# Expert numbers worked out on GpSimd between its gathers, in a two-layer trunk with product-key experts

## The chip, the cores and the metric

One core of a Trainium2 chip runs the whole program. The metric is the device time of one execution in microseconds. Of the kernel before there are three timed runs: 5895.33 us is their median, 5893.27 the lowest and 5913.72 the highest.

## The reference

Two layers run over 640 tokens (128 context, 512 latent) of width 1024. Each layer mixes tokens in four branches, merges them with gates, and then runs a retrieval of experts, which is the part that matters here:

```
q    = h @ w_q                                  # 8 heads, two halves of 128 each
sc   = scores of each half against 128 keys
s_half, i_half = top_k(sc, 16)                  # per half: 16 values and their key numbers
cand = s_half[0][:, None] + s_half[1][None, :]  # 256 sums a head
top_s, top_pos = top_k(cand, 16)
eidx = i_half[0][top_pos // 16] * 128 + i_half[1][top_pos % 16]
gate = softmax(top_s)
out  = sum_k gate_k * gelu(u_tab[eidx_k] . h) * v_tab[eidx_k]
```

A token so reads 8 x 16 = 128 rows of the two tables (16384 rows, stored side by side, 8 KB a row).

## The kernel before, in words

Everything is float32. Tokens lie in five tiles of 128, tile 0 being the context; tiles 0 and 1 form chunk 0, tiles 2 to 4 chunk 1. The gates, the output projection and the expert scores are done for chunk 0 first and then for chunk 1 (second gates pass, score stretch). An expert group has 2 slots in chunk 0 and 4 in chunk 1.

A slot is one gather: one expert row for each of the 128 tokens of a tile, 1 MB, into one of up to 15 places of the ring `ring[...]` in SBUF. There are 5 x 128 = 640 slots a layer. GpSimd issues them in order (line 444), each behind a wait that its place is free: places used by TensorE come free with `pe_used`, those used by VectorE with `dve_used`. The ring has 6 places at first, more from slots 132, 236, 352, 400 and 528 on (`LATER`, line 101). Slots are used in groups (`GROUPS`, line 80): of a group VectorE forms all products with the hidden row (`products`, line 1394), ScalarE applies the gelu (line 862), VectorE multiplies the gates in (`weights`, line 1414), and the weighted sum is then made by TensorE with diagonal matrices (line 476, made by ScalarE in line 868) for all but the last slot of a group, and by VectorE for the last (`sums`, line 1426).

Before a tile's slots can be gathered, its 8 heads must be selected on VectorE. `select(t, i)` (line 1382) does part i % 4 of head i // 4: `half_tops` (the best 16 of both halves), `pair_tops` (the best 16 of 256 sums), `places` (gates' exponents, the two halves of the position, and the comparison of each with the list 0..15), `numbers` (the multiplication by the key numbers, the reduction, and the expert's number into `EI`). The last signals `ei_ok`, on which GpSimd waits once for each 16 slots.

The parts lie in the order of work as follows. Tile 0's heads come one after another, between copies of two score rounds each (lines 1464 to 1469). Tile 1's parts follow one by one behind each pair of expert groups in the second gates pass (`select(1, s)`, line 1477), while tile 0's rows are gathered and used, with weight loads on SP's queue beside them. Tile 2's parts lie in the score stretch (lines 1493 to 1502):

```
experts(AT_KEYS + hp * KEY_STEP)
if hp:     score_copy(1, hp - 1); v.drain()
if hp >= 2: select(2, hp * KEY_STEP - 4)
experts(AT_KEYS + hp * KEY_STEP + 1)
if hp >= 2: select(2, hp * KEY_STEP - 3)
```

and the last head's four parts stand together behind it (line 1507). In that stretch TensorE does the queries of a round (line 533), one expert group, the key scores of the round before (line 541) and a second expert group (lines 799 to 804). Parts of tiles 3 and 4 lie one behind each expert group of tiles 2 and 3. Places 7 to 11 of the ring are first used once the last scores are copied (`pq_s`, line 440).

Of the kernel before, what the change touches and what calls it, by code (L numbers as in the profile page):

```python
# [16 lines left out]
ALU = mybir.AluOpType  # L17
ACT = mybir.ActivationFunctionType
AX = mybir.AxisListType

P = 128
# [17 lines left out]
PH = 8  # L39
# [75 lines left out]


HOME, BEFORE = rows_in_ring()
TURN = [HOME[:n].count(HOME[n]) for n in range(TILES * SLOTS)]
TURNS = [HOME.count(s) for s in range(HOMES)]

# [41 lines left out]
def program(nc, ws, cst, tabs, masks, ppd, cvec, rowd, fing, skd, kcd, vcd, tables, xin,  # L162
            y_out, nk_out):
    with ExitStack() as ctx:
# [64 lines left out]

        KS = [A[:, 0:2048], A[:, 2048:4096], B2[:, 2048:4096], B2[:, 4096:6144], R[:, 0:2048]]  # L230
        small = Small(A[:, 6144:6144 + SMALL])
        diag = [A[:, 7424 + i * P:7424 + (i + 1) * P] for i in range(DIAGS)]
        acc = A[:, 8192:9216]
        wgt = A[:, 10368:10624]
# [86 lines left out]
        pq_q = sig("pq_q", 2 * UNITS)  # L321
        pq_sp = sig("pq_sp", 2 * UNITS)
        pq_s = sig("pq_s", 2 * UNITS, 2)
        ei_ok = sig("ei_ok", TILES * PH)
        got = [sig(f"got{b}", 16 * TURNS[b]) for b in range(HOMES)]
        g_exp = sig("g_exp", TILES)
# [69 lines left out]
        @block.gpsimd  # L396
        def _(pool):
            for l in range(0, DEPTH):
                pool.wait_ge(layer_done.sem, layer_done.at(l, 0))
                pool.memset(convh, 0.0)  # L400
                pool.memset(V[:, 5, :], 0.0).then_inc(pads.sem, 1)

                pool.wait_ge(fo_ops.sem, fo_ops.at(l, CJ))
                pool.memset(kTw[:, :, 5 * P:6 * P], 0.0).then_inc(pads.sem, 1)


                def queries(n):
                    flat = A[:, 4352:10752]
                    pool.tensor_copy(QN[0], flat[:, bass.ds(n * 1280 + 640, 512)])
                    pool.tensor_copy(QN[1], flat[:, bass.ds(n * 1280, 512)]).then_inc(qs_ok.sem, 1)  # L410


                pool.wait_ge(kq_ok.sem, kq_ok.at(l, 1))
                pool.wait_ge(ln_n.sem, ln_n.at(l, 1))
                queries(0)
                for n in range(1, TILES):
                    pool.wait_ge(qt_ps.sem, qt_ps.at(l, n))
                    queries(n)


                for n in range(TILES * SLOTS):
                    s, b = HOME[n], BEFORE[n]
                    if n % TOPK == 0:
                        pool.wait_ge(ei_ok.sem, ei_ok.at(l, n // TOPK + 1))
                    if b in PE_AT:
                        pool.wait_ge(pe_used.sem, pe_used.at(l, PE_AT[b] + 1))
                    elif b in DVE_AT:
                        pool.wait_ge(dve_used.sem, dve_used.at(l, DVE_AT[b] + 1))
                    elif s == 3:

                        pool.wait_ge(pq_s.sem, pq_s.at(l, UNITS))
                    elif s == 5:

                        pool.wait_ge(ei_ok.sem, ei_ok.at(l, PH))
                    elif s == 6:

                        pool.wait_ge(ei_ok.sem, ei_ok.at(l, 2 * PH))
                    elif s == 7:

                        pool.wait_ge(pq_s.sem, pq_s.at(l, 2 * UNITS))  # L440
                    elif s >= 12:

                        pool.wait_ge(ei_ok.sem, ei_ok.at(l, (s - 9) * PH))
                    pool.indirect_dma_start(  # L444
                        out=ring[s], out_offset=None, in_=tables[:, :],
                        in_offset=bass.IndirectOffsetOnAxis(ap=EI[:, n:n + 1], axis=0),
                    ).then_inc(got[s].sem, 16)
# [365 lines left out]
        def _(act):  # L813
# [39 lines left out]
            def experts(l, q):  # L853

                g = GROUPS[q]
                if g.place == 0:
                    act.wait_ge(ei_ok.sem, ei_ok.at(l, (g.tile + 1) * PH))
                    gates = GT[:, g.tile * SLOTS:(g.tile + 1) * SLOTS]
                    act.activation(gates, gates, ACT.Exp).then_inc(g_exp.sem, 1)
                c, w = g.slots[0] % (2 * SLOTS), len(g.slots)  # L860
                act.wait_ge(u_done.sem, u_done.at(l, q + 1))
                act.activation(gel[:, c:c + w], dots[:, c:c + w], ACT.Gelu_apprx_tanh).then_inc(u_act.sem, 1)  # L862
                act.wait_ge(wgt_ok.sem, wgt_ok.at(l, q + 1))
                for n in g.pe:
                    p, o = PE_AT[n], n % (2 * SLOTS)

                    act.wait_ge(pe_used.sem, pe_used.at(l, p + 1 - DIAGS))
                    act.activation(diag[p % DIAGS], ident, ACT.Copy, scale=wgt[:, o:o + 1]).then_inc(diag_ok.sem, 1)  # L868
# [180 lines left out]
        def _(v):  # L1049
# [35 lines left out]
            for l in range(0, DEPTH):  # L1085
# [254 lines left out]

                def pair_tops(w, t, h):

                    v.tensor_copy(w.sf, w.si)
                    v.tensor_tensor(out=w.cand.rearrange("p (a b) -> p a b", a=TOPK),
                                    in0=w.sv[:, 0, :].unsqueeze(2).broadcast_to([P, TOPK, TOPK]),
                                    in1=w.sv[:, 1, :].unsqueeze(1).broadcast_to([P, TOPK, TOPK]), op=ALU.add)
                    v.drain()
                    top16([w.cand], [w.tv], [w.ti])

                full = [P, 2, TOPK, TOPK]  # L1350

                def places(w, t, h):

                    v.tensor_scalar(out=GT[:, bass.ds(t * SLOTS + h * TOPK, TOPK)], in0=w.tv, scalar1=w.tv[:, 0:1], scalar2=None,
                                    op0=ALU.subtract)

                    v.tensor_scalar(out=w.pu[:, 0, :], in0=w.ti, scalar1=TOPK * (TOPK - 1), scalar2=None, op0=ALU.bitwise_and)
                    v.tensor_scalar(out=w.pu[:, 1, :], in0=w.ti, scalar1=TOPK - 1, scalar2=None, op0=ALU.bitwise_and)
                    v.drain()
                    v.tensor_copy(w.pf, w.pu)  # L1360
                    v.drain()
                    v.tensor_tensor(out=w.EQ, in0=w.pf.unsqueeze(3).broadcast_to(full),
                                    in1=io[:, 0:2 * TOPK].rearrange("p (c a) -> p c a", c=2).unsqueeze(2).broadcast_to(full),
                                    op=ALU.is_equal)
                    v.drain()

                def numbers(w, t, h):

                    v.tensor_tensor(out=w.EQ, in0=w.EQ, in1=w.sf.unsqueeze(2).broadcast_to(full), op=ALU.mult)
                    v.drain()  # L1370
                    v.tensor_reduce(out=w.ef, in_=w.EQ, axis=AX.X, op=ALU.add)
                    v.drain()

                    v.scalar_tensor_tensor(out=w.er, in0=w.ef[:, 0, :], scalar=float(P), in1=w.ef[:, 1, :], op0=ALU.mult, op1=ALU.add)
                    v.drain()
                    v.tensor_scalar(out=EI[:, bass.ds(t * SLOTS + h * TOPK, TOPK)], in0=w.er,
                                    scalar1=io[:, bass.ds(l + 2 * TOPK, 1)], scalar2=None, op0=ALU.add)
                    v.drain().then_inc(ei_ok.sem, 1)  # L1378

                parts = (half_tops, pair_tops, places, numbers)  # L1380

                def select(t, i):

                    if i < 4 * PH:
                        parts[i % 4](small, t, i // 4)

                def products(q):

# [239 lines left out]
```

## Time and profile before

| | |
|---|---|
| median of three runs | 5895.33 us |
| profiled execution | 5903.82 us, span 5902.0 us |
| TensorE busy | 4460.0 us (76%) |
| VectorE busy | 3760.7 us (64%) |
| ScalarE busy | 870.3 us (15%) |
| GpSimd busy | 1581.7 us (27%), 1280 gathers among it |
| gathers on the DMA engines | 1342.26 MB, 56.7% of 16 engines' span |
| loads on the DMA engines | 240.02 MB, 10.9% |
| mean granted TensorE clock | 0.875 |

Busy times are shares of the whole span, and the phases of the kernel have different limits, so the table alone does not say what a change in one phase is worth. The idle time in front of an instruction stands in brackets in the listings, with what ended it. The clock is given as a share of full speed.

### The profile page before, as it was taken

To read this page: it belongs to the slowest core of one execution; us is meant where nothing else is said; L and a number is where in the kernel's file an instruction comes from. 1 tells how busy PE (TensorE), PEld (TensorE's weight loads), DVE (VectorE), ACT (ScalarE), POOL (GpSimd) and SP (SyncE) were. 2 spreads that over 40 slices of the span, in tenths; PEclk is the share of its full clock that TensorE was granted. 3 is DMA by queue.
4 is the path that set the end of the run, shared out by engine and by line. 5 is a ranking of instruction groups with operands and counts; after the bars stand their busy time and mean duration, and the time that the engine had idled before them with its cause. 6 is when DMAs were issued, how large, how long until landed. Compare 5 with 4: busy or idle time off the path is not lost.

```text
span 5902.0 us, 46602 instructions
## 1 busy us (share of the span) xinstructions
PE 4460.0 (76%) x14496; PEld 2588.8 (44%) x14496; DVE 3760.7 (64%) x8187; ACT 870.3 (15%) x2476; POOL 1581.7 (27%) x1310
## 2 busy tenths in 40 slices
PE   5999997888755666666669999968887556666665
PEld 3766685444432222222238667854444322222222
DVE  0655316688666888886607553177885668888765
ACT  1023201111100111111110232101111001111111
POOL 0000000333312544445300000013432234444453
PEclk8999898999877788888879999989998778888887
DMA  6100143899965999999851001439998669999996
GB/s 239 58 29 1 34 146 119 337 379 373 357 232 209 421 421 421 421 420 422 334 223 50 29 1 62 146 142 363 375 366 322 233 244 421 421 421 421 420 421 287
DMA packets 226377, 1585.27 MB, mean 269 GB/s; under 512 B 26064, under 2 KB 28368, under 8 KB 46672
## 3 DMA queue, kind: packets, MB, share of 16 engines
q0 software_dynamic: 184320, 1342.26, 56.7%
q1 hardware_dynamic: 41808, 240.02, 10.9%
q8 instruction: 116, 1.90, 0.1%
q14 instruction: 133, 1.09, 0.0%
HBM read 1579.03 MB, written 3.15 MB: 268 GB/s over the span
## 4 chain that ended last, share of the span: by engine, by line
PE 42%; DMA 33%; DVE 17%; issue 3%; ACT 3%; DVEq 2%; POOL 1%; SPq 0%; ACTq 0%; POOLq 0%
DMA B<-tables,R 19%; PE ps L476 9%; DMA A<-tables,R 6%; PE ps L486 5%; PE ps L596 5%; DMA H<-tables,R 4%; DVE A L1426 4%; DVE B L1394 4%; PE ps L533 3%; DMA B<-ws 3%; PE ps L581 2%; PE ps L493 2%; PE ps L506 2%; PE ps L701 2%; PE ps L688 2%
## 5 line engine op out<-in xcount | busy, mean ns | idle before, releaser
L476 PE MATMUL ps<-B,A 128*128 128x512 f32 x1928 | 1124.1, 730 | 663.0 <-ACT A L868 662.8
L444 POOL DMA_INDIRECT B<-tables,R x716 | 859.1, 1200 | 1932.4 <-DVEq L1378 740.3
L1394 DVE SCALAR_TENSOR_TENSOR B<-B,M 128x1024 f32<-128x1024 f32 x716 | 867.2, 1225 | 292.5 <-DMA B<-tables,R 263.8
L476 PEld LDWEIGHTS ps<-B,A 128*128 128x128 f32 x1928 | 422.1, 230 | 1285.0 <-ACT A L868 788.4
L476 PE MATMUL ps<-A 128*128 128x512 f32 x896 | 524.7, 723 | 253.7 <-ACT A L868 253.7
L486 PE MATMUL ps<-H,B 128*128 128x384 f32 (+1 forms) x2048 | 595.3, 445 | 62.9 <-DMA B<-ws 42.0
L444 POOL DMA_INDIRECT A<-tables,R x356 | 443.5, 1246 | 681.8 <-PE ps L476 372.0
L486 PEld LDWEIGHTS ps<-H,B 128*128 128x128 f32 x2048 | 400.0, 196 | 254.5 <-DMA B<-ws 47.0
L1394 DVE SCALAR_TENSOR_TENSOR A<-A,M 128x1024 f32<-128x1024 f32 x356 | 433.4, 1224 | 116.3 <-DMA A<-tables,R 103.9
L862 ACT ACTIVATE T<-T 128x2 f32<-128x2 f32 (+1 forms) x448 | 91.6, 204 | 2531.5 <-DVEq L1396 2531.5
L476 PEld LDWEIGHTS ps<-A 128*128 128x128 f32 x896 | 201.3, 234 | 534.8 <-ACT A L868 307.9
L476 PE MATMUL ps<-H,A 128*128 128x512 f32 x456 | 275.1, 735 | 154.8 <-ACT A L868 154.8
L868 ACT ACTIVATE A<-cs,A 128x128 f32<-128x128 f32 x832 | 292.1, 394 | 591.8 <-DVEq L1415 591.8
L444 POOL DMA_INDIRECT H<-tables,R x192 | 239.5, 1248 | 491.4 <-DVE A L1426 185.0
L1426 DVE SCALAR_TENSOR_TENSOR A<-B,A 128x1024 f32<-128x1024 f32 x230 | 295.4, 1284 | 30.8 <-issue 1.5
L533 PE MATMUL ps<-H,B 128*128 128x256 f32 (+1 forms) x1024 | 310.5, 460 | 2.2 <-ACT M L840 2.2
L493 PE MATMUL ps<-B 128*128 128x256 f32 (+1 forms) x1024 | 297.7, 434 | 0.0
L1394 DVE SCALAR_TENSOR_TENSOR H<-H,M 128x1024 f32<-128x1024 f32 x192 | 235.1, 1225 | 74.5 <-DMA H<-tables,R 68.9
L596 PE MATMUL ps<-B,H 128*128 128x256 f32 x1280 | 276.8, 379 | 3.7 <-DVE M L1131 3.7
L533 PEld LDWEIGHTS ps<-H,B 128*128 128x128 f32 x1024 | 211.2, 209 | 115.0 <-issue 43.8
L596 PEld LDWEIGHTS ps<-B,H 128*128 128x128 f32 x1280 | 243.0, 190 | 37.9 <-DVE M L1131 4.9
L493 PEld LDWEIGHTS ps<-B 128*128 128x128 f32 x1024 | 195.5, 191 | 96.4 <-issue 32.6
(206 smaller groups left out, 5111.1 us busy)
## 6 DMA issues: line engine op xcount, KB each, us to landing
B<-ws SPq DMA_DIRECT2D x120, 1024.0 KB, 6.9
B<-ws SPq DMA_DIRECT2D x128, 768.0 KB, 7.8
B<-tables,R POOLq DMA_INDIRECT x716, 18.7
A<-tables,R POOLq DMA_INDIRECT x356, 14.0
R<-tabs SPq DMA_DIRECT2D x2, 2176.0 KB, 8.9
H<-tables,R POOLq DMA_INDIRECT x192, 17.0
x<-xin SPq DMA_DIRECT2D x1, 2560.0 KB, 9.3
y<-M SPq DMA_DIRECT2D x1, 2560.0 KB, 7.9
```

The source lines that it names most:

```text
L444: pool.indirect_dma_start(out=ring[s], out_offset=None, in_=tables[:, :], in_offset=bass.IndirectOffsetOnAxis(ap=EI[:, n:n + 1], axis=0),) ...
L476: mm = pe.matmul(ps[:, bk + c, :], diag[PE_AT[n] % DIAGS], v_row[:, c * 512:(c + 1) * 512], start=(n % SLOTS == 0), stop=(PE_AT[n] + 1 == ...
L486: last = pe.matmul(ps[:, bk, 0:WIDTH[c]], w[:, k * P:(k + 1) * P], h[:, k, :], start=(k == 0), stop=(k == KD - 1))
L493: last = pe.matmul(ps[:, bk, 0:WIDTH[c]], w[:, (KD + k) * P:(KD + k + 1) * P], br[:, s % 4, k, :], start=(k == 0), stop=(k == CJ - 1))
L506: last = pe.matmul(ps[:, bk + part // 2, (part % 2) * 256:(part % 2 + 1) * 256], mTc[c][:, k, i * P:(i + 1) * P], w[:, k * 256:(k + 1) * 2 ...
L533: last = pe.matmul(ps[:, hp % 2, 0:WIDTH[c]], w[:, o:o + P], hTc[c][:, k, :], start=(k == 0), stop=(k == KD - 1))
L581: last = pe.matmul(ps[:, bk + 2 * c + bank, 0:WIDTH[bank]], home(AT_CP + j)[:, k * 256 + c * P:k * 256 + c * P + P], hTc[bank][:, k, :], s ...
L596: last = pe.matmul(ps[:, g % 4, 0:256], hTc[CHUNK[t]][:, k, PLACE[t]:PLACE[t] + P], home(AT_QP + q * WS + s)[:, k * 256:(k + 1) * 256], st ...
L688: return pe.transpose(ps[:, bank, o * P:(o + 1) * P], Pb[u % 2][:, i * P:(i + 1) * P], ident)
L868: act.activation(diag[p % DIAGS], ident, ACT.Copy, scale=wgt[:, o:o + 1]).then_inc(diag_ok.sem, 1)
L1394: v.scalar_tensor_tensor(out=u_row, in0=u_row, scalar=1.0, in1=h2[:, g.tile, :], op0=ALU.mult, op1=ALU.mult, accum_out=dots[:, o:o + 1])
L1426: last = v.scalar_tensor_tensor(out=acc, in0=v_row, scalar=wgt[:, o:o + 1], in1=acc, op0=ALU.mult, op1=ALU.add)
```

## The change

The comparison, the multiplication, the reduction and the last two steps of a head move from VectorE to GpSimd. VectorE now writes the key numbers and the two halves of the position, as floats, into one of four copies of a small buffer (`halves`, `places`, chosen by h % 4) and signals `gt_ok`. GpSimd's `numbers(t, h)` waits for it, makes a difference and a comparison with zero in place of the comparison, multiplies, adds in a tree of four steps in place of the reduction, forms the number in three small steps, and signals `ei_ok`. VectorE waits before it overwrites a copy that GpSimd may still read. `NUMBERS_AT` says before which slot of GpSimd's loop a head stands: tile 0's heads 0 to 5 ahead of slot 0, heads 6 and 7 ahead of slot 3, tile 1's head h ahead of slot 20 + 16h, tile 2's ahead of 192 + 8h, tile 3's ahead of 288 + 16h, tile 4's ahead of 416 + 16h. The four parts of a head become two, at even i, and the odd calls of `select` do nothing.

```diff
@@ -115,6 +115,12 @@
 HOME, BEFORE = rows_in_ring()
+
+
+NUMBERS_AT = {3: [6, 7]}
+for _k in range(PH, TILES * PH):
+    _t, _h = divmod(_k, PH)
+    NUMBERS_AT.setdefault(192 + 8 * _h if _t == 2 else (_t - 1) * SLOTS + TOPK * _h + (20 if _t == 1 else 32), []).append(_k)
 TURN = [HOME[:n].count(HOME[n]) for n in range(TILES * SLOTS)]
 TURNS = [HOME.count(s) for s in range(HOMES)]
@@ -229,6 +235,8 @@
         KS = [A[:, 0:2048], A[:, 2048:4096], B2[:, 2048:4096], B2[:, 4096:6144], R[:, 0:2048]]
         small = Small(A[:, 6144:6144 + SMALL])
+        halves = [T[:, 512 + i * 32:544 + i * 32].rearrange("p (c k) -> p c k", c=2) for i in range(4)]
+        places = [A[:, 10624 + i * 32:10656 + i * 32].rearrange("p (c k) -> p c k", c=2) for i in range(4)]
         diag = [A[:, 7424 + i * P:7424 + (i + 1) * P] for i in range(DIAGS)]
         acc = A[:, 8192:9216]
         wgt = A[:, 10368:10624]
@@ -321,6 +329,7 @@
         pq_q = sig("pq_q", 2 * UNITS)
         pq_sp = sig("pq_sp", 2 * UNITS)
         pq_s = sig("pq_s", 2 * UNITS, 2)
+        gt_ok = sig("gt_ok", TILES * PH)
         ei_ok = sig("ei_ok", TILES * PH)
         got = [sig(f"got{b}", 16 * TURNS[b]) for b in range(HOMES)]
         g_exp = sig("g_exp", TILES)
@@ -418,8 +427,39 @@
                     queries(n)
+                full = [P, 2, TOPK, TOPK]
+
+                def numbers(t, h):
+
+                    w = small
+                    pool.wait_ge(gt_ok.sem, gt_ok.at(l, t * PH + h + 1))
+                    pool.tensor_tensor(out=w.EQ, in0=places[h % 4].unsqueeze(3).broadcast_to(full),
+                                       in1=io[:, 0:2 * TOPK].rearrange("p (c a) -> p c a", c=2).unsqueeze(2).broadcast_to(full),
+                                       op=ALU.subtract)
+                    pool.drain()
+                    pool.tensor_scalar(out=w.EQ, in0=w.EQ, scalar1=0.0, scalar2=None, op0=ALU.is_equal)
+                    pool.drain()
+                    pool.tensor_tensor(out=w.EQ, in0=w.EQ, in1=halves[h % 4].unsqueeze(2).broadcast_to(full), op=ALU.mult)
+                    for n in (8, 4, 2):
+                        pool.drain()
+                        pool.tensor_tensor(out=w.EQ[:, :, :, 0:n], in0=w.EQ[:, :, :, 0:n], in1=w.EQ[:, :, :, n:2 * n], op=ALU.add)
+                    pool.drain()
+                    pool.tensor_tensor(out=w.ef, in0=w.EQ[:, :, :, 0], in1=w.EQ[:, :, :, 1], op=ALU.add)
+                    pool.drain()
+                    pool.tensor_scalar(out=w.er, in0=w.ef[:, 0, :], scalar1=float(P), scalar2=io[:, 2 * TOPK + l:2 * TOPK + l + 1],
+                                       op0=ALU.mult, op1=ALU.add)
+                    pool.drain()
+                    pool.tensor_tensor(out=w.er, in0=w.er, in1=w.ef[:, 1, :], op=ALU.add)
+                    pool.drain()
+                    pool.tensor_copy(EI[:, t * SLOTS + h * TOPK:t * SLOTS + (h + 1) * TOPK], w.er)
+                    pool.drain().then_inc(ei_ok.sem, 1)
+
+                for h in range(6):
+                    numbers(0, h)
                 for n in range(TILES * SLOTS):
                     s, b = HOME[n], BEFORE[n]
+                    for k in NUMBERS_AT.get(n, ()):
+                        numbers(k // PH, k % PH)
                     if n % TOPK == 0:
                         pool.wait_ge(ei_ok.sem, ei_ok.at(l, n // TOPK + 1))
                     if b in PE_AT:
@@ -431,16 +471,16 @@
                         pool.wait_ge(pq_s.sem, pq_s.at(l, UNITS))
                     elif s == 5:
-                        pool.wait_ge(ei_ok.sem, ei_ok.at(l, PH))
+                        pool.wait_ge(gt_ok.sem, gt_ok.at(l, PH))
                     elif s == 6:
-                        pool.wait_ge(ei_ok.sem, ei_ok.at(l, 2 * PH))
+                        pool.wait_ge(gt_ok.sem, gt_ok.at(l, 2 * PH))
                     elif s == 7:
                         pool.wait_ge(pq_s.sem, pq_s.at(l, 2 * UNITS))
                     elif s >= 12:
-                        pool.wait_ge(ei_ok.sem, ei_ok.at(l, (s - 9) * PH))
+                        pool.wait_ge(gt_ok.sem, gt_ok.at(l, (s - 9) * PH))
                     pool.indirect_dma_start(
                         out=ring[s], out_offset=None, in_=tables[:, :],
                         in_offset=bass.IndirectOffsetOnAxis(ap=EI[:, n:n + 1], axis=0),
@@ -854,7 +894,7 @@
                 g = GROUPS[q]
                 if g.place == 0:
-                    act.wait_ge(ei_ok.sem, ei_ok.at(l, (g.tile + 1) * PH))
+                    act.wait_ge(gt_ok.sem, gt_ok.at(l, (g.tile + 1) * PH))
                     gates = GT[:, g.tile * SLOTS:(g.tile + 1) * SLOTS]
                     act.activation(gates, gates, ACT.Exp).then_inc(g_exp.sem, 1)
                 c, w = g.slots[0] % (2 * SLOTS), len(g.slots)
@@ -1340,49 +1380,40 @@
                 def pair_tops(w, t, h):
-                    v.tensor_copy(w.sf, w.si)
+                    if t * PH + h >= 4:
+                        v.wait_ge(ei_ok.sem, ei_ok.at(l, t * PH + h - 3))
+                    v.tensor_copy(halves[h % 4], w.si)
                     v.tensor_tensor(out=w.cand.rearrange("p (a b) -> p a b", a=TOPK),
                                     in0=w.sv[:, 0, :].unsqueeze(2).broadcast_to([P, TOPK, TOPK]),
                                     in1=w.sv[:, 1, :].unsqueeze(1).broadcast_to([P, TOPK, TOPK]), op=ALU.add)
                     v.drain()
                     top16([w.cand], [w.tv], [w.ti])
-                full = [P, 2, TOPK, TOPK]
-
-                def places(w, t, h):
-
-                    v.tensor_scalar(out=GT[:, bass.ds(t * SLOTS + h * TOPK, TOPK)], in0=w.tv, scalar1=w.tv[:, 0:1], scalar2=None,
-                                    op0=ALU.subtract)
-
+                def scaled(w, t, h):
+
+                    v.tensor_scalar(out=GT[:, t * SLOTS + h * TOPK:t * SLOTS + (h + 1) * TOPK], in0=w.tv, scalar1=w.tv[:, 0:1],
+                                    scalar2=None, op0=ALU.subtract)
                     v.tensor_scalar(out=w.pu[:, 0, :], in0=w.ti, scalar1=TOPK * (TOPK - 1), scalar2=None, op0=ALU.bitwise_and)
                     v.tensor_scalar(out=w.pu[:, 1, :], in0=w.ti, scalar1=TOPK - 1, scalar2=None, op0=ALU.bitwise_and)
                     v.drain()
-                    v.tensor_copy(w.pf, w.pu)
-                    v.drain()
-                    v.tensor_tensor(out=w.EQ, in0=w.pf.unsqueeze(3).broadcast_to(full),
-                                    in1=io[:, 0:2 * TOPK].rearrange("p (c a) -> p c a", c=2).unsqueeze(2).broadcast_to(full),
-                                    op=ALU.is_equal)
-                    v.drain()
-
-                def numbers(w, t, h):
-
-                    v.tensor_tensor(out=w.EQ, in0=w.EQ, in1=w.sf.unsqueeze(2).broadcast_to(full), op=ALU.mult)
-                    v.drain()
-                    v.tensor_reduce(out=w.ef, in_=w.EQ, axis=AX.X, op=ALU.add)
-                    v.drain()
-
-                    v.scalar_tensor_tensor(out=w.er, in0=w.ef[:, 0, :], scalar=float(P), in1=w.ef[:, 1, :], op0=ALU.mult, op1=ALU.add)
-                    v.drain()
-                    v.tensor_scalar(out=EI[:, bass.ds(t * SLOTS + h * TOPK, TOPK)], in0=w.er,
-                                    scalar1=io[:, bass.ds(l + 2 * TOPK, 1)], scalar2=None, op0=ALU.add)
-                    v.drain().then_inc(ei_ok.sem, 1)
-
-                parts = (half_tops, pair_tops, places, numbers)
+                    v.tensor_copy(places[h % 4], w.pu)
+                    v.drain().then_inc(gt_ok.sem, 1)
+
+                def first_half(w, t, h):
+
+                    half_tops(w, t, h)
+
+                def second_half(w, t, h):
+
+                    pair_tops(w, t, h)
+                    scaled(w, t, h)
+
+                parts = (first_half, second_half)
                 def select(t, i):
-                    if i < 4 * PH:
-                        parts[i % 4](small, t, i // 4)
+                    if i < 4 * PH and i % 2 == 0:
+                        parts[i // 2 % 2](small, t, i // 4)
                 def products(q):
```

## Rows read from the trace of the kernel before

**Rows 1.** Busy time by stretch: us; PE, PEld, DVE, ACT, POOL; clock, DMA, GB/s.

```profile
926.00:1018.00 92.00, 65.99 (x279) 53.34 (x278) 78.94 (x306) 7.33 (x16) 5.84 (x6) 0.85 0.26 100
1100.00:1460.00 360.00, 318.08 (x876) 162.59 (x874) 299.86 (x634) 50.16 (x141) 145.83 (x112) 0.99 0.97 376
1588.00:1888.00 300.00, 186.66 (x481) 98.91 (x479) 188.98 (x470) 26.72 (x79) 65.77 (x65) 0.77 0.68 242
...
1920.00:2930.00 1010.00, 678.77 (x1175) 266.75 (x1174) 784.40 (x1605) 127.86 (x409) 491.28 (x397) 0.83 1.00 417
```

**Rows 2.** Timeline, tile 0's selection and what follows: start, length, instruction [idle before].

```profile
933.89 0.69 DVE L1362 TENSOR_TENSOR A<-A,io 128x512 f32<-128x512 f32 x1
...
936.79 0.76 DVE L1311 COPY A<-ps 128x256 f32<-128x256 f32 x2
936.99 1.11 POOL L444 DMA_INDIRECT B<-tables,R  x1 [375.63 <-DVEq L1378]
...
938.40 0.94 POOL L444 DMA_INDIRECT B<-tables,R  x1 [0.30 <-issue]
...
1006.53 0.94 POOL L444 DMA_INDIRECT H<-tables,R  x1 [65.95 <-DVE A L1311]
...
1021.02 3.78 PE L476 MATMUL ps<-B,A 128*128 128x512 f32 x4 [6.55 <-ACT A L868]
...
1036.58 8.38 PE L486 MATMUL ps<-H,B 128*128 128x384 f32 x16 [7.06 <-DMA B<-ws]
```

**Rows 3.** GpSimd's groups over the whole span: busy us, mean ns, idle before.

```profile
L409 POOL COPY T<-A 128x512 f32<-128x512 f32 x10 | 6.1, 611 | 310.8 <-PE ps L658 310.8
...
L401 POOL MEMSET A<- 128x256 f32 x2 | 0.6, 307 | 0.0
...
L1620 POOL MEMSET const-uint8-127<- 128x1 uint8 x1 | 0.1, 119 | 0.0
```

**Rows 4.** DMA issues from 1100, 1588 and 1920 us on: median us to landing.

```profile
B<-tables,R POOLq DMA_INDIRECT x56, 9.4
...
B<-tables,R POOLq DMA_INDIRECT x28, 5.9
...
B<-tables,R POOLq DMA_INDIRECT x243, 21.2
```

**Rows 5.** Timeline in the gates pass, a gather and a product.

```profile
1149.62 1.23 DVE L1394 SCALAR_TENSOR_TENSOR B<-B,M 128x1024 f32<-128x1024 f32 x1
1149.69 1.96 POOL L444 DMA_INDIRECT B<-tables,R  x1 [4.01 <-DVE A L1426]
```

**Rows 6.** Timeline of the score stretch, then the chain's first and last rounds.

```profile
1662.01 0.29 DVE L1337 COPY A<-B 128x256 f32<-128x256 f32 x1
...
1665.94 1.23 DVE L1394 SCALAR_TENSOR_TENSOR B<-B,M 128x1024 f32<-128x1024 f32 x1
...
1670.32 3.78 PE L476 MATMUL ps<-B,A 128*128 128x512 f32 x4 [9.07 <-ACT A L868]
...
1673.25 1.23 DVE L1394 SCALAR_TENSOR_TENSOR A<-A,M 128x1024 f32<-128x1024 f32 x1
...
1679.13 1.88 PE L476 MATMUL ps<-A 128*128 128x512 f32 x4
...
1682.44 0.23 DVE L1354 TENSOR_SCALAR R<-A 128x16 f32<-128x16 f32 x1
...
1683.93 1.23 DVE L1394 SCALAR_TENSOR_TENSOR B<-B,M 128x1024 f32<-128x1024 f32 x1
...
1688.31 3.78 PE L476 MATMUL ps<-B,A 128*128 128x512 f32 x4 [6.63 <-ACT A L868]
...
1903.42 1.96 POOL L444 DMA_INDIRECT H<-tables,R  x1 [15.37 <-DVE A L1426]
```

**Rows 7.** The chain of waits: start us, us, what.

```profile
1609.80 3.78 PE ps L476 x4
...
1883.07 3.78 PE ps L476 x4
```

## Prediction

> **What bounds the kernel now.** I read the stretches between the kernel's phases first, then the chain of waits, then the order of instructions where the places and numbers are worked out, and last GpSimd's own rows. The first layer falls into parts with different limits, and the second repeats them.
>
> [rows 1] is the table by stretch. From 926 to 1018 us VectorE selects the experts of tile 0 and does little else: it is busy 79 of 92 us and the DMA engines are a quarter used. From 1100 to 1460 us (second gates pass, rows of tile 0 gathered beside it) the DMA share is 0.97. From 1588 to 1888 us (query and key scores of tiles 2 to 4) nothing is full: TensorE is busy 187 of 300 us, VectorE 189, the DMA share is 0.68, GpSimd is busy 66. From 1920 to 2930 us the DMA share is 1.00. So work taken from VectorE can pay in the first and the third stretch and in the gap before the last, while in the other two VectorE has slack and what matters is that the queue of gathers never runs dry.
>
> **Part 1: tile 0's selection, VectorE relieved.** In [rows 2] the comparison with the list of places starts at 933.89 and the next score copy at 936.79, so 2.90 us of a head lie between them. All of it goes (multiply, reduction, combination, addition and their drains) but about 0.1 us of closing drain: 2.8 us a head. Head 0 ends at about 936.7, and head 6 at 1005.5, 1 us before GpSimd's issue at 1006.53 that its score copy releases, so a head takes 11.5 us and head 7 ends near 1016.7; the products, the activation and the weights stand between it and TensorE's first expert matmul at 1021.02. So 8 x 2.8 = 22 us a layer is the most that this part gives. TensorE needs two score rounds for each head, which at the pace of the other heads still leaves VectorE the later one.
>
> GpSimd's chain for a head now stands behind it. No row of before has it: ten instructions and ten drains. I bound one by the nearest rows [rows 3]: a copy of 512 elements took 0.61 us, a fill of 256 took 0.31 us, a fill of one element 0.12 us. Every operation at the price of a copy or a fill: 3 x 0.61 for the 512-wide ones, 0.31 for the sum of 256, about 0.2, 0.16 and 0.13 for 128, 64 and 32, and 3 x 0.12 for the last three: 3.0 us, the low end. If an operation with two inputs costs twice its one-input price: 2 x 1.22 + 0.61 + 0.61 + 0.98 + 0.48 = 5.1 us, and ten drains at the 0.30 us that separate two gathers with nothing to wait for (938.40 in [rows 2]) add 3.0: 8.1 us, the high end. I take 6.5 us, inside the upper half, because adds with two inputs are most of it. The Trainium skill, "GPSIMD Engine Reference", section 3.1, gives about 2.6 cycles an element for an addition of two tensors, at 1.2 GHz. No row here has such an addition. By the page the two 512-wide ones take 1.1 us each and the chain an estimated 4.2 us without drains, 7.2 with them as above, and the sum below would be some 12 us higher.
>
> With 6.5 us GpSimd keeps up with a head every 8.7 us. The order is numbers of heads 0 to 5, then gathers 0 to 2, then numbers of heads 6 and 7, then gather 3. Gather 0 went out at 936.99 before; now it follows head 5, which ends at 933.9 + 5 x 8.7 = 977, so at about 984, and with the 5.9 us landing of a quiet queue [rows 4] it is there when VectorE ends its selection at 1016.7 - 22 = 995. Gather 3 goes out at about 1002 (995 + 6.5 and the issue) instead of 1006.53, but now 7 us behind the selection instead of 10 ahead. What hides this is the second weight load of the pass: TensorE sat 7.06 us before 1036.58 for weights [rows 2], and those steps take 20 us each. So I keep most of the gain: -18 us a layer, bounds -22 (all hidden) to +5 (a chain of 10 us, gathers 0 and 3 both late).
>
> **Part 2: the gates pass with tile 0's rows.** Eight chains stand here between gathers, one each 16 rows. A chain beside expert work is longer than a quiet one: in [rows 5] a gather that starts 0.07 us after VectorE's 1.23 us product takes 1.96 us, while an undisturbed one takes 0.94. Over the stretch a gather takes 145.83 / 112 = 1.30 us [rows 1], so 0.36 us of waiting each; ten instructions at that rate make 6.5 + 3.6 = 10 us. The Trainium skill, "SBUF — State Buffer", section "Who interferes with whom", has VectorE and GpSimd lock a shared port pair for whole instructions. The 1.96 us row agrees. The page adds the inference that a two-input operation leaves a gather's descriptors alone, since it takes only the read side; the row does not bear that out. By the lock GpSimd's reads would hold VectorE up in turn, which speaks against this change.
>
> Behind the chain stand the gathers. GpSimd is idle 214 us over 112 gathers here, about 2 us each [rows 1], which covers a first part. A gather lands 9.4 us after its issue here and 5.9 us where the queue is short [rows 4], so 3.5 us of queued work cover a second. Left are 10 - 2 - 3.5 = 4.5 us; the weight loads on SP's queue fill some, and the mean share was 0.97 and not 1. I take 3 us a head: +24 us a layer. Ends: a chain of 6.5 us costs nearly nothing and a freed VectorE may close the missing 3% of DMA share (-11 us of 360); without cover 8 x 8.5 = +68.
>
> **Part 3: the score stretch, where work moves onto the path.** This is where I expect the edit to lose although it removes work. `select` is called twice a score round, once between the score copy and the second expert group, once behind that group. Before, the calls alternated: half tops in the first place and pair tops in the second, next round places in the first and numbers in the second. Now i % 2 == 0 works only, so each first place is filled (half tops; next round pair tops with the scaling) and the second is empty. [rows 6] shows which place counts. Half tops ran from 1662.01 to 1665.94, 3.93 us, and TensorE sat 9.07 us before 1670.32 for the weights behind it. Places ran 1682.44 to 1683.93, 1.49 us, and there TensorE sat 6.63 us before 1688.31. The second place is covered: pair tops ended before the product at 1673.25, its weights came about 4 us on (two products, the activation, a sum), and TensorE reached its expert matmul only at 1679.13, out of its queries. So the 3.3 us of pair tops and 2.1 of numbers that leave the second place were free, and the first place of every other round grows from 1.49 us to 3.33 + 0.74 = 4.07 us (0.74 from 1682.44 to the comparison, with its drain). That is +2.6 us for each of seven heads. The chain's rounds bear it out: from 1609.80 to 1883.07 in 14 rounds is 19.5 us a round [rows 7], and those behind half tops measure 20.6 against 18.5. I take +2.3 x 7 = +16 and another +3 for VectorE held up by a chain (0.4 a head): +19 a layer. Ends: 0 (if TensorE's clock, 0.77 of full here, hides it) and +30.
>
> **Part 4: behind it.** Head 7 of tile 2 is selected alone, in one piece; GpSimd waited 15.37 us for what follows [rows 6]. Here 2.8 us go: -3 us a layer. In the last stretch gathers land 21.2 us after issue [rows 4], 15 us over the quiet 5.9, and a chain of 6.5 + 10 x 0.3 = 9.5 us fits under it; GpSimd goes from 491 to about 730 busy of 1010 us. VectorE, 784 of 1010, gives 3 us a head and may lose as much to the shared port. I cost this at +1 a layer for the first refill, 0 to +20.
>
> **The sum.** -18 + 24 + 19 - 3 + 1 = +23 us a layer, +46 for two. Made against the profiled execution (span 5902.0, 5903.82 us in all), 8 us over the median of 5895.33, it gives 5950 there and 5941 at the median; I say 5940. A measurement here tells about 0.5% (29 us) from no change.
>
> **Rivals.**
> (a) The chain is short, 6.5 us also beside expert work, as the low half of the bounds allows. Then part 2 is about +4, the others stay: -20 + 4 + 17 - 3 = -2 a layer, 5891 at the median. For it: the 0.61 us copy. Against it: the 1.96 us gathers. Chance 0.28.
> (b) Faster. VectorE's relief counts in the gates pass as well, since the chain there passes through VectorE's sums at each slot's release, and sooner releases keep the queue full; part 2 is -11, part 3 only +5, if the end of the second place counts in a part of the rounds. -22 - 11 + 5 - 3 = -31 a layer, 5833. It decides if the DMA share between 1100 and 1460 rises to 1. Against it: 0.97 leaves little. Chance 0.14.
> (c) GpSimd becomes the bound. Its chain costs 13 us alone (slow on four-dimensional operands, dear drains) and 17 beside expert work. Tile 0's first group waits for the gathers (part 1: +20), part 2 is 8 x (17 - 5.5) = +92, part 3 +19: +130 a layer, 6155. Chance 0.13.
> (d) The forecast, 5905 to 5985. Chance 0.45.
>
> **The numbers.** Faster by over 0.5% is (b) and a little of (a): 0.16. Within it, most of (a) and the low end of (d): 0.30. Slower: 0.54. The range leaves out (c) and part of (b): 5850 to 6060; my own case alone is 5905 to 5985.
>
> **What would show it.** Right: VectorE's busy time falls by some 210 us (80 heads at 2.7) and the time does not follow; tile 0's selection is about 20 us shorter a layer; rounds of the score stretch are all near 20.6 us; GpSimd's chain takes 6 to 7 us in tile 0's selection and about 10 beside expert work; the DMA share from 1100 to 1460 has dips after rows 20, 36, 52. Wrong: score rounds that still alternate, a DMA share that holds at 0.97 with the eight chains inside, or a chain outside 4 to 12 us.

## The result, and the profile after

The changed kernel takes 6557.55 us (median of 4 runs, 6554.42 to 6559.93) against 5894.3 us before (5884.88 to 5913.72). The recorded ratio of the runs is 1.1107, 95% interval 1.1085 to 1.1129; here and below it can differ from the quotient of the two medians by up to 0.002. It is 663 us slower, where 46 were forecast. Its profiled execution spans 6556.3 us, 654 more than before.

The page of the changed kernel, engines and the DMA share in 40 slices:

```profile
PE 4530.2 (69%) x14496; PEld 2622.2 (40%) x14496; DVE 3665.6 (56%) x7787; ACT 874.7 (13%) x2476; POOL 2088.0 (32%) x2110
DMA  5100337888656777779951003278786577777798
```

VectorE's busy time fell by 95 us, and no engine is near full. TensorE is busy 70 us longer at a mean granted clock of 0.832 of full, after 0.875; how much of the loss passes through that was not measured separately. What fell clearly is the DMA share: where it stood at 9 it stands at 7. By stretch, in the columns of [rows 1]:

```profile
925.00:1016.00 91.00, 69.85 (x317) 56.09 (x315) 65.84 (x274) 9.55 (x21) 52.44 (x79) 0.90 0.28 99
1100.00:1460.00 360.00, 280.09 (x718) 143.68 (x717) 238.81 (x485) 40.05 (x115) 148.44 (x145) 0.89 0.83 321
...
1960.00:2900.00 940.00, 487.66 (x836) 193.66 (x834) 594.20 (x1283) 89.91 (x286) 439.83 (x456) 0.74 0.77 313
```

The gates pass has a DMA share of 0.83 after 0.97, and the last stretch, where chains stand ahead of tiles 3 and 4, has 0.77 after 1.00.

GpSimd alone shows why. First a quiet chain in tile 0's selection, no gather before it (timeline, the columns of [rows 2]):

```profile
937.68 1.05 POOL L436 TENSOR_TENSOR A<-A,io 128x512 f32<-128x512 f32 x1 [372.66 <-DVEq L1400]
938.91 1.50 POOL L440 TENSOR_SCALAR A<-A 128x512 f32<-128x512 f32 x1 [0.17 <-issue]
940.56 1.27 POOL L442 TENSOR_TENSOR A<-A,T 128x512 f32<-128x512 f32 x1
941.97 1.83 POOL L445 TENSOR_TENSOR A<-A 128x256 f32<-128x256 f32 x3
943.95 0.24 POOL L447 TENSOR_TENSOR A<-A 128x32 f32<-128x32 f32 x1
944.36 0.28 POOL L449 TENSOR_SCALAR A<-A,io 128x16 f32<-128x16 f32 x1 [0.17 <-issue]
944.78 0.22 POOL L452 TENSOR_TENSOR A<-A 128x16 f32<-128x16 f32 x1
945.14 0.20 POOL L454 CAST R<-A 128x16 int32<-128x16 f32 x1
```

It takes 7.7 us from 937.68 to 945.34, and the gap at each drain is 0.1 to 0.2 us. Then a chain in the last stretch, with gathers ahead of it:

```profile
2213.03 1.94 POOL L484 DMA_INDIRECT A<-tables,R  x1 [0.78 <-PE ps L516]
2215.27 1.11 POOL L484 DMA_INDIRECT B<-tables,R  x1 [0.30 <-issue]
2216.40 1.06 POOL L436 TENSOR_TENSOR A<-A,io 128x512 f32<-128x512 f32 x1
2232.12 2.26 POOL L440 TENSOR_SCALAR A<-A 128x512 f32<-128x512 f32 x1 [14.66 <-issue]
...
2239.03 0.20 POOL L454 CAST R<-A 128x16 int32<-128x16 f32 x1
2240.11 1.03 POOL L484 DMA_INDIRECT B<-tables,R  x1 [0.89 <-POOLq L455]
```

Between the difference and the comparison stands one drain, and it took 14.66 us. The DMA engines in the same microseconds (busy time by window; the last two numbers are DMA share and GB/s):

```profile
2224.00:2228.00 4.00, 3.31 (x4) 1.50 (x5) 3.41 (x15) 0.99 (x3) 0.00 (x0) 0.50 1.00 418
2228.00:2230.00 2.00, 2.00 (x4) 0.69 (x3) 1.82 (x4) 0.00 (x0) 0.00 (x0) 0.50 0.71 295
2230.00:2231.00 1.00, 1.00 (x3) 0.49 (x2) 1.00 (x3) 0.00 (x0) 0.00 (x0) 0.61 0.06 25
2231.00:2232.00 1.00, 1.00 (x3) 0.38 (x2) 1.00 (x3) 0.00 (x0) 0.00 (x0) 1.00 0.00 0
...
2238.00:2240.00 2.00, 2.00 (x7) 0.79 (x5) 0.00 (x0) 0.00 (x0) 0.77 (x4) 1.00 0.00 0
2240.00:2242.00 2.00, 0.58 (x2) 0.00 (x0) 0.00 (x0) 0.00 (x0) 1.59 (x2) 1.00 0.22 29
```

GpSimd goes on at 2232.12, about 1 us after the last bytes have moved. The queue is empty by 2231, the chain's remaining 7 us follow with idle DMA engines, and data moves again from about 2241: some 10 us of nothing, in a stretch that was full before. The group's row over the whole span:

```profile
L440 POOL TENSOR_SCALAR A<-A 128x512 f32<-128x512 f32 x80 | 154.3, 1928 | 805.8 <-issue 805.8
```

Fourteen of the 80 heads have no gather between the chain before and their own (tile 0's heads 0 to 5 and 7, in both layers); the other 66 hold nearly all of the 805.8 us, 12.2 each.

To place the time I measure four stretches of each layer by first and last starts in the trace: S1 from tile 0's first score copy to the first expert matmul, S2 from there to the last output projection, S3 from the first to the last score copy of chunk 1, S4 from there to the last expert matmul. In us, first / second layer, from the profiled execution; the last column is the median of the timed runs:

| kernel | S1 | S2 | S3 | S4 | median |
|---|---|---|---|---|---|
| before | 99 / 99 | 513 / 519 | 284 / 280 | 1057 / 1056 | 5894 |
| changed | 79 / 82 | 610 / 615 | 313 / 313 | 1275 / 1271 | 6558 |
| semaphores (e1) | 78 / 78 | 558 / 564 | 308 / 309 | 1064 / 1064 | 6010 |
| drain alone (e2) | 99 / 99 | 546 / 541 | 281 / 280 | 1150 / 1144 | 6141 |
| first drain (e10) | 80 / 81 | 599 / 605 | 312 / 316 | 1256 / 1261 | 6504 |
| semaphores, four places (e4) | 78 / 78 | 557 / 557 | 292 / 292 | 1066 / 1068 | 5987 |
| before, two places (e5) | 99 / 99 | 544 / 544 | 319 / 320 | 1056 / 1054 | 6040 |
| tile 0 only (e7) | 78 / 78 | 513 / 516 | 282 / 279 | 1055 / 1056 | 5849 |
| behind second group (e8) | 99 / 99 | 512 / 511 | 259 / 260 | 1055 / 1055 | 5855 |
| e7 and e8 (e9) | 78 / 78 | 514 / 511 | 259 / 262 | 1056 / 1055 | 5810 |
| e7 with fills (e11) | 78 / 78 | 539 / 537 | 283 / 279 | 1055 / 1055 | 5907 |

The changed kernel against before: S1 -37 us for both layers together, S2 +193, S3 +62, S4 +433; together 651 of the 654.

### The profile page after: what moved, and what is told of

Same layout as the page of the kernel before. It is cut to its first block, busy times and chain, and to the rows that moved or that the text cites. A ratio compares the mean times of both kernels' runs of the same rounds, so it can differ in the third digit from the quotient of the medians.

```text
span 6556.3 us, 47404 instructions
## 1 busy us (share of the span) xinstructions
PE 4530.2 (69%) x14496; PEld 2622.2 (40%) x14496; DVE 3665.6 (56%) x7787; ACT 874.7 (13%) x2476; POOL 2088.0 (32%) x2110
## 4 chain that ended last, share of the span: by engine, by line
issue 28%; PE 26%; DMA 19%; DVE 12%; POOLq 7%; POOL 5%; ACT 2%; DVEq 2%; SPq 0%; ACTq 0%
DMA B<-tables,R 9%; PE ps L516 8%; PE ps L636 4%; DMA A<-tables,R 4%; DVE A L1457 3%; POOLq L444 3%; DMA H<-tables,R 3%; DVE B L1425 2%; POOL B L484 2%; PE ps L573 2%; PE ps L621 2%; POOLq L441 2%; DMA B<-ws 2%; POOLq L439 1%; DVE A L1425 1%
## 5 line engine op out<-in xcount | busy, mean ns | idle before, releaser
L516 PE MATMUL ps<-B,A 128*128 128x512 f32 x1928 | 1150.2, 745 | 1000.0 <-ACT A L908 986.3
L484 POOL DMA_INDIRECT B<-tables,R x716 | 829.0, 1158 | 839.8 <-PE ps L516 454.1
L484 POOL DMA_INDIRECT A<-tables,R x356 | 415.6, 1167 | 495.2 <-PE ps L516 262.0
L526 PEld LDWEIGHTS ps<-H,B 128*128 128x128 f32 x2048 | 398.9, 195 | 237.2 <-issue 44.6
L440 POOL TENSOR_SCALAR A<-A 128x512 f32<-128x512 f32 x80 | 154.3, 1928 | 805.8 <-issue 805.8
L1457 DVE SCALAR_TENSOR_TENSOR A<-B,A 128x1024 f32<-128x1024 f32 x230 | 314.1, 1365 | 29.8
L436 POOL TENSOR_TENSOR A<-A,io 128x512 f32<-128x512 f32 x80 | 88.6, 1108 | 742.8 <-DVEq L1400 740.3
L533 PE MATMUL ps<-B 128*128 128x256 f32 (+1 forms) x1024 | 313.2, 450 | 0.0
L484 POOL DMA_INDIRECT H<-tables,R x192 | 224.1, 1167 | 276.1 <-DVE A L1457 136.1
L516 PEld LDWEIGHTS ps<-H,A 128*128 128x128 f32 x456 | 106.3, 244 | 440.6 <-ACT A L908 322.9
```

Source lines behind the costliest of these rows:

```text
L440: pool.tensor_scalar(out=w.EQ, in0=w.EQ, scalar1=0.0, scalar2=None, op0=ALU.is_equal)
L484: pool.indirect_dma_start(out=ring[s], out_offset=None, in_=tables[:, :], in_offset=bass.IndirectOffsetOnAxis(ap=EI[:, n:n + 1], axis=0),) ...
L516: mm = pe.matmul(ps[:, bk + c, :], diag[PE_AT[n] % DIAGS], v_row[:, c * 512:(c + 1) * 512], start=(n % SLOTS == 0), stop=(PE_AT[n] + 1 == ...
L526: last = pe.matmul(ps[:, bk, 0:WIDTH[c]], w[:, k * P:(k + 1) * P], h[:, k, :], start=(k == 0), stop=(k == KD - 1))
L533: last = pe.matmul(ps[:, bk, 0:WIDTH[c]], w[:, (KD + k) * P:(KD + k + 1) * P], br[:, s % 4, k, :], start=(k == 0), stop=(k == CJ - 1))
L1457: last = v.scalar_tensor_tensor(out=acc, in0=v_row, scalar=wgt[:, o:o + 1], in1=acc, op0=ALU.mult, op1=ALU.add)
```

## The experiments

Each ratio is to the kernel before as timed beside it: a median of 5897.86 us for e1, e2, e4 and e5, 5888.59 for e7 to e10, 5902.51 for e11. The edits are shortened; the text says against which kernel each stands.

**e1: semaphores instead of drains.** The changed kernel, but each GpSimd instruction of the chain raises a semaphore, and the next waits for it.

```diff
-pool.tensor_tensor(out=w.EQ, ..., op=ALU.subtract)
-pool.drain()
-pool.tensor_scalar(out=w.EQ, in0=w.EQ, scalar1=0.0, ..., op0=ALU.is_equal)
+step(pool.tensor_tensor(out=w.EQ, ..., op=ALU.subtract))        # .then_inc(nm.sem, 1)
+settled()                                                       # pool.wait_ge(nm.sem, steps[0])
+step(pool.tensor_scalar(out=w.EQ, in0=w.EQ, scalar1=0.0, ..., op0=ALU.is_equal))
```

> The changed kernel with GpSimd's ten drains a head replaced by semaphores that its own instructions raise and wait for; work, places and order are the same. Theory A (a drain on GpSimd waits until every gather issued before it has landed, so each of the 64 heads inside the stream of gathers empties the DMA queue): the idle time in front of the comparison, 10.1 us a head in the changed kernel, falls under 0.5 us, and the time comes down from 6558 to 5900 to 5980 us. Theory B (GpSimd's 7.7 us of work a head, lengthened by VectorE, is what holds the gathers back): the work stays, so the time stays above 6300 us.

Measured: 6009.88 us, ratio to before 1.0185 (1.0158 to 1.0211). 548 of the 663 us are gone. The comparison's group in this kernel (columns of [rows 3]) shows the idle time that is left:

```profile
L451 POOL TENSOR_SCALAR A<-A 128x512 f32<-128x512 f32 x80 | 152.7, 1909 | 7.4
```

It is 7.4 us in place of 805.8, with the same instructions. S4 is back to within 8 us of before. Theory A holds for the cause; the time lies 30 us above its range, and what is left (+112 us over before) has other causes.

**e2: the drain alone.** The kernel before, all on VectorE, with a bare drain.

```diff
 s, b = HOME[n], BEFORE[n]
+if n in NUMBERS_AT:
+    pool.drain()
```

> The kernel before with one bare drain on GpSimd ahead of the same slots (3, 20, 36, ..., 528), 33 a layer, and nothing else. Theory A: each drain holds the next gather until the queue is empty, some 8 us in the second gates pass and 15 us in the last stretch, and the DMA engines then idle about 3 us before the next gather's packets: 66 x 3 = +200 us, 6050 to 6150 us. Theory B: a drain alone costs nothing, 5880 to 5910 us.

Measured: 6140.81 us, ratio 1.0416 (1.0393 to 1.0439), as theory A had it. GpSimd in the last stretch of this kernel, and the windows there:

```profile
2301.35 1.12 POOL L451 DMA_INDIRECT A<-tables,R  x1 [0.30 <-issue]
2320.39 0.94 POOL L451 DMA_INDIRECT H<-tables,R  x1 [17.93 <-issue]
```

```profile
2311.00:2318.00 7.00, 5.82 (x10) 2.64 (x11) 5.54 (x13) 0.99 (x3) 0.00 (x0) 0.76 0.93 385
2318.00:2322.00 4.00, 1.24 (x3) 0.19 (x1) 2.81 (x5) 0.42 (x2) 1.30 (x2) 1.00 0.02 6
```

With nothing to compute, a drain still holds GpSimd for 17.93 us, until the queue is empty. So 243 us come from 66 drains by themselves, 3.7 each; in the changed kernel some 7 us of chain follow behind the empty queue (windows above), and replacing its drains is worth 8.3 us for each of the 66 (548 / 66).

**e10: only the first drain replaced,** in the changed kernel.

```diff
-pool.tensor_tensor(out=w.EQ, ..., op=ALU.subtract)
-pool.drain()
+pool.tensor_tensor(out=w.EQ, ..., op=ALU.subtract).then_inc(nm.sem, 1)
+pool.wait_ge(nm.sem, steps[0])
```

> The changed kernel with only the first of a chain's ten drains replaced by a semaphore. Theory A (any GpSimd drain waits for all gathers issued before it): the 10 us of idle time move from in front of the comparison to in front of the multiplication and the time is that of the changed kernel, 6530 to 6570 us. Rival (the wait belongs to the first arithmetic instruction behind a gather, a change of program on GpSimd, and not to the drain): it goes with the first drain, or stays in front of the comparison.

Measured: 6504.07 us. The first three steps of the chain in this kernel, difference (L438), comparison (L443) and multiplication (L445):

```profile
L443 POOL TENSOR_SCALAR A<-A 128x512 f32<-128x512 f32 x80 | 153.9, 1923 | 7.4
L445 POOL TENSOR_TENSOR A<-A,T 128x512 f32<-128x512 f32 x80 | 135.4, 1692 | 669.3 <-issue 667.4
...
L438 POOL TENSOR_TENSOR A<-A,io 128x512 f32<-128x512 f32 x80 | 88.3, 1104 | 743.6 <-DVEq L1403 741.1 <-issue 1.3
```

The wait moved with the drain, from the comparison to the multiplication. It belongs to whichever drain comes first behind gathers. It shrank by 138 us, 2.1 a head, which fits the comparison (1.9 us), now run while the gathers land. The time fell by 53 us, to 26 us under the expected range.

**e4: select's parts in their old places.** e1, with pair tops back behind the second group.

```diff
-parts = (first_half, second_half)
-if i < 4 * PH and i % 2 == 0:
-    parts[i // 2 % 2](small, t, i // 4)
+parts = (half_tops, pair_tops, scaled)
+if i < 4 * PH and i % 4 < 3:
+    parts[i % 4](small, t, i // 4)
```

> As the kernel with semaphores, but select's parts keep their old places: half tops, pair tops, scaling, nothing, so that pair tops leave the first place of a score round. Theory of the prediction's part 3: against the kernel with semaphores and two parts, the score stretch is 7 x 3.3 us shorter a layer at most, the time 35 to 50 us lower, about 5880. Rival: the place does not matter since VectorE's sum is the same, within 10 us of the kernel with two parts.

Measured: 5986.66 us, 23 less than e1, under the 35 expected, and 107 above the 5880 of the expectation, which leaned on a lower e1. S3 gives 16.5 us a layer (308 to 292), which is 2.4 for each of seven heads; I had counted all 3.3 of pair tops. S2 does not change in the first layer and is 7 us shorter in the second.

**e5: the old kernel with two places.** All on VectorE, half tops at i % 4 == 0, and pair tops, places and numbers together at i % 4 == 2.

```diff
-if i < 4 * PH:
-    parts[i % 4](small, t, i // 4)
+if i < 4 * PH and i % 2 == 0:
+    for part in ((half_tops,), (pair_tops, places, numbers))[i // 2 % 2]:
+        part(small, t, i // 4)
```

> The kernel before (all on VectorE) with its four parts in two calls: half tops, then pair tops with places and numbers, the odd calls empty. It tests part 3 of the prediction by itself. By it the first place of every other round of the score stretch grows from 1.5 to 6.9 us, +5.4 x 7 x 2 = +76 us less what cover there is: 5950 to 5975 us. Rival (VectorE's place in the round is covered either way): 5885 to 5905 us.

Measured: 6040.05 us, ratio 1.0248 (1.0223 to 1.0273), 65 us over the expected range. The score stretch did as expected (S3 +36 and +40 a layer against 38). The rest is S2, +31 and +25: in the gates pass too one lump of 6.9 us costs more than its parts spread out. The cause of that stays open; in e1, whose largest lump is 4.1 us, spreading it (e4) left S2 at 557 in both layers.

**e7: tile 0 alone on GpSimd,** with semaphores; tiles 1 to 4 as before. Against the kernel before:

```diff
+NUMBERS_AT = {3: [6, 7]}                       # and numbers(t, h) of e1
 ...
 # VectorE, after the two halves of the position:
+if t == 0:
+    v.tensor_copy(places[h % 4], w.pu)
+    v.drain().then_inc(gt_ok.sem, 1)
+    return
```

> Semaphores instead of drains, and GpSimd works out the numbers of tile 0 alone; tiles 1 to 4 stay on VectorE in the four parts of the kernel before. Theory: tile 0's part is the only gain of the change (18.4 us a layer in the kernel with semaphores) and the gates pass (+45), the score stretch (+24) and the last stretch (+7) go back to before: 5897 - 37 = 5860 us, 5850 to 5875. Rival: two chains behind slot 2 delay the first steps of the gates pass as much, so that nothing is left: 5890 to 5900.

Measured: 5848.64 us, ratio 0.9927 (0.9906 to 0.9948), as the theory had it, 1 us under its range. S1 keeps its 21 us a layer and S2 to S4 are those of before.

**e8: tile 2's selection behind the second expert group.** The kernel before, all on VectorE.

```diff
-if hp >= 2: select(2, hp * KEY_STEP - 4)          # between the groups
 experts(AT_KEYS + hp * KEY_STEP + 1)
-if hp >= 2: select(2, hp * KEY_STEP - 3)
+if hp >= 2:
+    for i in ((1, 2, 3) if hp % 2 else (0,)):
+        select(2, (hp - 2) // 2 * 4 + i)
```

> The kernel before, all on VectorE, with the parts of tile 2 taken out of the first place of a score round: half tops behind the second expert group of even rounds, the other three parts behind that of odd rounds. By part 3's reading of the rounds (the first place is on the path, the second covered by TensorE's queries up to 4.8 us in one round and 6.7 in the next), 3.9 + 1.5 us a head leave the path and 0.2 come on: -5 x 7 x 2 = -70 us at most; 5830 to 5870. Rival (other waits take their place in the round, and the gathers behind): within 15 us of before.

Measured: 5854.92 us, ratio 0.9937 (0.9915 to 0.9959), inside the expected range. S3 is 25 and 20 us shorter, of the 35 a layer that were the most.

**e9: e7 and e8 together.**

> Tile 0 alone on GpSimd by semaphores, and tile 2's parts behind the second expert group. The two gains lie in different stretches, so they add: the sum of what the two kernels with one edit each gain, 5790 to 5840 us if both hold. Rival: the last stretch, full in DMA, takes one of them back.

Measured: 5810.07 us, ratio 0.9865 (0.9841 to 0.9888): the two gains add (0.9927 x 0.9937 = 0.9864), and S4, full in DMA, takes nothing back. It is the fastest kernel of all here, 79 us under the one before.

**e11: GpSimd held up without reading,** in the kernel of e7.

```diff
 s, b = HOME[n], BEFORE[n]
+if n in range(20, 133, 16):
+    for _ in range(32):
+        settled()
+        step(pool.memset(A[:, 10624:10752], 0.0))
```

> The kernel with tile 0 alone on GpSimd, and in the gates pass, at the slots of tile 1's heads (20, 36, ..., 132), 32 fills of 128 elements on GpSimd, each behind a semaphore: about 10 us of GpSimd time a head that reads nothing from SBUF and changes no work of VectorE. It asks what the 45 us a layer of the gates pass consist of, which the kernel with semaphores has too much. If it is GpSimd's time alone, which holds the next gather (11.5 us a head there), the gates pass grows by 35 to 45 us a layer, 5925 to 5940 us in all. If VectorE, held up by GpSimd's reads, is the cause, it grows by less than 10 us a layer: 5850 to 5870 us.

Measured: 5906.52 us, ratio 1.0013 (0.9996 to 1.003). One chain of fills and the two gathers around it:

```profile
1177.55 1.42 POOL L495 DMA_INDIRECT H<-tables,R  x1 [3.04 <-DVE A L1488]
1178.97 8.36 POOL L471 MEMSET A<- 128x128 f32 x32
1187.49 0.95 POOL L495 DMA_INDIRECT B<-tables,R  x1 [0.15 <-issue]
```

It fell between the two expectations; the fills took 8.4 us and not 10, and VectorE's products stayed at 1.225 us, as in e7, so the fills held up GpSimd alone. S2 grew by 26 and 21 us against e7, so 3 us a head; 5.4 of the 8.4 us were covered. The chain of e1 takes 11.5 us there: 11.5 - 5.4 = 6.1, times 8 heads = 49 us, and e1's S2 has 45. So GpSimd's time in front of the next gather is enough to explain the gates pass, without VectorE's longer instructions, whose share was not measured by itself.

## Why the prediction was wrong

**The step that failed is the price of the drains in part 1.** I wrote "ten drains at the 0.30 us that separate two gathers with nothing to wait for" and took the chain's high end from it. A drain behind a computation costs 0.1 to 0.2 us, so the number is not the error. The error is that I gave drains one price wherever they stand. Behind gathers the first one waits for all that are under way: 12.2 us for each of 66 heads, and the chain, bounded at 3.0 to 8.1 us, blocks the queue for all of it. The kernel before has no drain on GpSimd, so no row showed this wait; what such a wait would cost could have been read from the 9.4 and 21.2 us to landing [rows 4]. Replacing the drains takes 548 us back (e1); nothing else that I named comes near.

**Part 4** therefore failed by the most. I said that a chain of 9.5 us "fits under" 15 us of queued gathers. With semaphores it does: S4 is +7 and +8 us in e1, where I had +1. With drains the queue is gone before the chain begins, so there is no cover, and S4 grew by 218 and 216 us.

**Part 1, apart from that, held in the main.** The chain measured 7.7 us against 6.5, inside the bounds; its operations with two inputs of 512 took 1.05 and 1.27 us. S1 shortened by 20 and 17 us, by 21 in e1; forecast 18. Gather 3 is another matter. I had it go out at 1002; in the changed kernel it stood behind a drain and two chains:

```profile
1003.55 1.50 POOL L440 TENSOR_SCALAR A<-A 128x512 f32<-128x512 f32 x1 [7.79 <-issue]
...
1018.62 1.03 POOL L484 DMA_INDIRECT H<-tables,R  x1 [0.82 <-issue]
...
1026.97 3.78 PE L516 MATMUL ps<-A 128*128 128x512 f32 x4 [15.69 <-ACT A L908]
...
1050.39 8.48 PE L526 MATMUL ps<-H,B 128*128 128x384 f32 x16 [7.44 <-DMA B<-ws]
```

From the first expert matmul (1004.69) to the second group of gate matmuls (the last line) 45.7 us pass, after 36.5 before; in the second layer 46.8 after 35.1. So 9 and 12 us of the gain in S1 are lost again in S2. In e7, without that drain, the same stretch takes 36.8 and 37.5 us: there the late gather is hidden behind the second weight load but for 2 us in the second layer.

**Part 2** was right in kind and too small. It costs 45 us a layer in e1, where I had 24. Its cover, 2 + 3.5 us, is what e11 measured (5.4). The chain beside expert work is 11.5 us and not 10, and I then rounded 4.5 us left down to 3 for the weight loads. (Its end of 8 x 8.5 us "without cover" does not follow: a chain of 10 us without cover is 8 x 10.) The last steps of the chain in the gates pass of e1 show what lengthens it:

```profile
1195.32 1.31 DVE L1435 SCALAR_TENSOR_TENSOR A<-A,M 128x1024 f32<-128x1024 f32 x1
...
1195.63 1.10 POOL L458 TENSOR_TENSOR A<-A 128x32 f32<-128x32 f32 x1
...
1196.57 1.25 DVE L1435 SCALAR_TENSOR_TENSOR H<-H,M 128x1024 f32<-128x1024 f32 x1
...
1196.83 1.13 POOL L460 TENSOR_SCALAR A<-A,io 128x16 f32<-128x16 f32 x1
...
1197.95 1.28 DVE L1467 SCALAR_TENSOR_TENSOR A<-B,A 128x1024 f32<-128x1024 f32 x1
1198.04 1.27 POOL L463 TENSOR_TENSOR A<-A 128x16 f32<-128x16 f32 x1
...
1199.38 0.20 POOL L465 CAST R<-A 128x16 int32<-128x16 f32 x1
```

Steps of 0.2 to 0.3 us in the quiet chain take 1.1 to 1.3 here, and each ends about 0.1 us after the VectorE product or sum beside it; the cast, beside neither, keeps its 0.20. So the wait is per instruction, and the small ones pay as much as the large. That fits the lock told in the Trainium skill, "SBUF — State Buffer", section "Who interferes with whom". VectorE pays too: its sums of the changed kernel average 1.36 us after 1.28, and in e1 its busy time is 3699.8 us. e7 takes 36 us off VectorE for 16 heads; 80 heads at that rate would leave 3580, so about 120 us were given back. Of these 86 stand in its products and sums, which take 2178.4 us in e1 and 2092.7 in e7; the rest was not placed. By the same reckoning (180 us off for 80 heads) the changed kernel gave 85 back, so VectorE's busy time fell by 95 us there and not by the 210 expected.

**Part 3 held.** Rounds of the score stretch got longer although VectorE does less in them: S3 +24 and +29 in e1 for 19 forecast. e4 shows the share of the places (16.5 us, for 16 taken), e5 the same effect alone (36 and 40 for 38), and e8 its reverse (-25 and -20, of 35).

**The rivals.** (a), a chain of 6.5 us beside expert work, is refuted by the 11.5 us there. (c), GpSimd becoming the bound, had the right sign. It names "dear drains", but inside a chain of 13 us that is as dear in quiet as anywhere, where the quiet one took 7.7; it has no loss behind the score stretch, where two thirds of it lie (433 of 651 us); and its 6155 us is 400 short. That the forecast had the right sign comes from parts 2 and 3; most of the loss is a wait that neither it nor a rival had. (b) is refuted: with VectorE relieved in the gates pass the DMA share fell, even in e1.

## What to carry to other kernels

A drain on GpSimd, where it also issues gathers, has to be priced by the transfers that are still under way, not by the instruction in front of it. Order its own instructions by a semaphore there, and hand it work only where its queue is empty or where the work is shorter than what the queued gathers cover. And before counting what leaves an engine, find which of its slots in a round are on the path: a shorter sum in a worse place was slower here.

## What the runs showed of the hardware

- GpSimd's drain returned in 0.1 to 0.2 us behind a computation, after 7.8 us behind three gathers in a quiet queue, after 14.66 and 17.93 us in the full one, each time 1 to 2 us after the DMA engines had gone idle; a wait for a semaphore raised by GpSimd's own instruction cost at most 0.1 us on average, behind gathers too (7.4 us for 80 in e1).
- In e11 fills on GpSimd, which read nothing, left VectorE's products at 1.225 us; in e1, with chains that read SBUF, they averaged 1.27 to 1.29 us.
- GpSimd, quiet, 128x512 float32: difference of two tensors 1.05 us, product 1.27, comparison with a constant (one input) 1.50, copy 0.61. The dearest had one input.
